# A two-block transformer on one core: where an expert's fetched rows are turned, and where the code behind a branch stands

## The reference, cut to what matters

```python
def moe_swiglu(xn, router, wg, wu, wd):
    t = xn.reshape(B * S, D)                              # 256 x 1024
    top_val, top_idx = lax.top_k((t @ router), TOP_K)      # 2 of 8 experts
    gates = jax.nn.softmax(top_val, axis=-1)
    combine = jnp.sum(jax.nn.one_hot(top_idx, N_EXPERTS) * gates[..., None], axis=1)
    for e in range(N_EXPERTS):                             # 1024 -> 3584 -> 1024
        out = out + combine[:, e:e + 1] * swiglu(t, wg[e], wu[e], wd[e])
    return out

def first_block(x, p, ...):
    for i in range(DEPTH):
        h = h + hybrid_mixer(rmsnorm(h, norm_mix[i]), ...)
        h = h + (swiglu(...) if i % 2 == 0 else moe_swiglu(rmsnorm(h, norm_ffn[i]), ...))
        gate = jax.nn.sigmoid(rmsnorm(h, ple_norm[i]) @ ple_gate[i])
        h = h + gate * (p[i] @ ple_proj[i])
    return rmsnorm(h, final_norm)

def second_block(x, mem, ...):
    for l in range(DEPTH):
        ...                      # block attention, a gated recurrence, memory attention
        x = x + y @ w_out[l]
    return x
```

## Time and profile before

| | |
|---|---|
| median of 3 runs | 1982.92 us (1981.67 to 1983.06) |
| the profiled execution | 1982.62 us |
| its span | 1980.8 us |
| mean granted TensorE clock | 0.993 |
| busy: PE, DVE, ACT | 1923.5, 1518.7, 1229.4 us |

### The profile page before, as it was taken

How to read it: one execution, slowest core, us unless ns; L and a number is a source line. 1 busy time by engine, 2 the same in 40 slices (tenths; PEclk the granted TensorE clock), 3 DMA queues, 4 the chain that set the end, 5 groups by cost and what they waited for, 6 DMA issues and landing times.

```text
span 1980.8 us, 26870 instructions
## 1 busy us (share of the span) xinstructions
PE 1923.5 (97%) x10275; PEld 1632.1 (82%) x10275; DVE 1518.7 (77%) x1478; ACT 1229.4 (62%) x1332; POOL 28.4 (1%) x28
## 2 busy tenths in 40 slices
PE   8999999999899999999999999999998999999999
PEld 7889998887687887878878788787886788887987
DVE  4675555656788888888888888888996865877576
ACT  4554445554677777777777777777776545354442
POOL 0000000000000000000000000000000000000000
PEclk9999999999999999999999999999999999999999
DMA  7717554532799999999999999999995552345321
GB/s 240 255 59 249 188 192 149 164 113 99 280 375 341 391 379 348 381 340 390 379 348 373 361 395 374 359 384 353 396 361 203 170 171 86 128 170 191 128 86 43
DMA packets 246211, 514.63 MB, mean 260 GB/s; under 512 B 12516, under 2 KB 59240, under 8 KB 246120
## 3 DMA queue, kind: packets, MB, share of 16 engines
q1 hardware_dynamic: 242936, 502.77, 70.4%
q0 software_dynamic: 2896, 10.49, 1.3%
q10 hardware_dynamic: 288, 0.11, 0.0%
HBM read 507.56 MB, written 5.77 MB: 259 GB/s over the span
## 4 chain that ended last, share of the span: by engine, by line
PE 81%; DVE 10%; ACT 3%; issue 3%; SPq 2%; DMA 1%; DVEq 0%; ACTq 0%
PE bank L725 25%; PE bank L727 25%; PE bank L726 25%; DVE low L1936 3%; PE bank L1145 1%; DVE low L2533 1%; PE bank L696 1%; PE bank L849 1%; ACT high L1417 1%; SPq L674 1%; SPq L635 1%; DVE at L2738 1%; PE bank L840 1%; ACT high L1620 1%; PE bank L818 1%
## 5 line engine op out<-in xcount | busy, mean ns | idle before, releaser
L2533 DVE TENSOR_TENSOR low<-raw,high 128x2048 fp32r<-128x2048 f32 x336 | 768.4, 2291 | 117.7 <-ACT high L1620 116.8
L1620 ACT ACTIVATE high<-raw 128x2048 fp32r<-128x2048 f32 x336 | 644.7, 1920 | 240.1 <-PE bank L727 238.3
L1936 DVE TENSOR_TENSOR low<-raw,high 128x2048 fp32r<-128x2048 f32 (+1 forms) x138 | 310.5, 2259 | 168.1 <-ACT high L1417 164.4
L1417 ACT ACTIVATE high<-raw 128x2048 fp32r<-128x2048 f32 (+1 forms) x138 | 260.7, 1894 | 167.8 <-PE bank L727 150.3
L725 PE MATMUL bank<-high,xg_hi 128*128 128x512 f32 x896 | 353.7, 395 | 2.7 <-DVE xg_lo L2516 2.3
L727 PE MATMUL bank<-high,xg_lo 128*128 128x512 f32 x896 | 349.5, 390 | 0.0
L726 PE MATMUL bank<-low,xg_hi 128*128 128x512 f32 x896 | 348.9, 389 | 0.0
L725 PE MATMUL bank<-high,xT_hi 128*128 128x512 f32 (+1 forms) x576 | 228.3, 396 | 8.5 <-issue 5.4
L727 PE MATMUL bank<-high,xT_lo 128*128 128x512 f32 (+1 forms) x576 | 222.2, 386 | 0.0
L726 PE MATMUL bank<-low,xT_hi 128*128 128x512 f32 (+1 forms) x576 | 221.8, 385 | 0.0
L725 PE MATMUL bank<-high,hT_hi 128*128 128x512 f32 x536 | 212.7, 397 | 0.0
(11 more groups left out here) (346 smaller groups left out, 2231.5 us busy)
## 6 DMA issues: line engine op xcount, KB each, us to landing
raw<-in_moe_w_gate SPq DMA_DIRECT2D x112, 1024.0 KB, 6.5
raw<-in_moe_w_up SPq DMA_DIRECT2D x112, 1024.0 KB, 6.8
raw<-in_moe_w_down SPq DMA_DIRECT2D x112, 1024.0 KB, 6.6
raw<-in_w_in SPq DMA_DIRECT2D x63, 1024.0 KB, 5.4
raw<-in_w_out SPq DMA_DIRECT2D x20, 1024.0 KB, 5.0
raw<-in_dense_w_gate SPq DMA_DIRECT2D x11, 1024.0 KB, 5.2
raw<-in_dense_w_up SPq DMA_DIRECT2D x11, 1024.0 KB, 5.3
raw<-in_dense_w_down SPq DMA_DIRECT2D x11, 1024.0 KB, 5.0
```

The costliest lines, as they stand in the source:

```text
L1417: act.activation(high[:, slot, 0:k * n], raw[:, raw_slot[piece], 0:k * n], ACT.Copy).then_inc(high_done, 1)
L1620: act.activation(high[:, k % PARTS, :], raw[:, slot, :], ACT.Copy).then_inc(s["high"], 1)
L1936: dve.tensor_tensor(low[:, slot, 0:k * n], src, high[:, slot, 0:k * n].bitcast(F32), ALU.subtract).then_inc(low_done, 1)
L2533: dve.tensor_tensor(low[:, k % PARTS, :], raw[:, at0 + k % slots, :], high[:, k % PARTS, :].bitcast(F32), ALU.subtract).then_inc(s["low"], 1)
```

## The change

The diff has two parts. In the path that fetches rows by DMA, PE turns the next expert's rows one product earlier, between gate 6 and up 6, into banks 1 and 3, which the odd groups' gate and up products use and which are free by then. ACT waits for up 6 (the last reader of the old `xg_hi`) before it writes the new one. Three semaphores of their own replace the shared counters, and an expert has eight turns instead of ten.

```diff
-    return 5 + j if j < GROUPS - 1 else (11 if is_last else 13)
+    return 5 + j if j < GROUPS - 1 or s["by_dma"] else (11 if is_last else 13)
...
-        moe_sems[0].update(turns=10, by_dma=True)
+        rows_turned, rows_high, rows_low = (sem("taken_rows_" + x) for x in ("turned", "high", "low"))
+        moe_sems[0].update(turns=8, by_dma=True)
...
                         if (what, j) == ("gate", 0):
-                            pe.wait_ge(s["tfree"], 1 + half if is_first else s["turns"] * e + 10 - s["turns"] + half)
+                            if is_first or not s["by_dma"]:
+                                pe.wait_ge(s["tfree"], 1 + half if is_first else s["turns"] * e + 10 - s["turns"] + half)
+                            else:
+                                pe.wait_ge(rows_low, 2 * e - 1 + half)
...
                     if j >= 1:
                         turn_hidden(j - 1)
+                    if j == GROUPS - 1 and not is_last and s["by_dma"]:
+                        turn_taken(e + 1)
                     product("up", j)
...
-                    if j == GROUPS - 1 and not is_last:
-                        if s["by_dma"]:
-                            turn_taken(e + 1, s, lambda a: turn_bank(11 + a))
-                        else:
-                            gather(e + 1, s, lambda a: turn_bank(11 + a))
+                    if j == GROUPS - 1 and not is_last and not s["by_dma"]:
+                        gather(e + 1, s, lambda a: turn_bank(11 + a))
...
-            def turn_taken(e, s, bank_for):
+            def turn_taken(e):
...
                 for a in range(2):
-                    b = bank_for(a)
+                    b = bank[1 + 2 * a]
...
-                    last.then_inc(s["tfull"], 1)
+                    last.then_inc(rows_turned, 1)
```

On ACT and DVE `gathered` takes the semaphores and banks as arguments:

```diff
                     if (what, j, half) == ("up", GROUPS - 1, 1) and not is_last:
-                        gathered(s, s["turns"] * e + 10, (7, 6))
+                        if s["by_dma"]:
+                            act.wait_ge(s["used"], first + PER_EXPERT * e + q + 1)
+                            gathered(rows_turned, 2 * e + 1, rows_high, (1, 3))
+                        else:
+                            gathered(s["tfull"], s["turns"] * e + 10, s["thigh"], (7, 6))
...
                     if (what, j, half) == ("up", GROUPS - 1, 1) and not is_last:
-                        gathered(s, 9 * e + 8, (7, 6))
+                        if s["by_dma"]:
+                            gathered(rows_high, 2 * e, rows_low, (1, 3))
+                        else:
+                            gathered(s["thigh"], 9 * e + 8, s["tfree"], (7, 6))
```

```diff
                 with pe.If(over < 1):
                     finish(moe_sems[0])
-                    embedding_in(1)
+                    after_experts()
                 with pe.Else():
...
-                    embedding_in(1)
+                    after_experts()
...
+            def after_experts():
+                embedding_in(1)
+                embedding_out(1)
+                for l in range(LAYERS):
+                    km, vm = ([(name, l, t) for t in range(NT)] for name in ("km", "vm"))
...
                 else:
                     experts()
-                embedding_out(l)
-
-            for l in range(LAYERS):
-                km, vm = ([(name, l, t) for t in range(NT)] for name in ("km", "vm"))
...
                 if l == 0:
+                    embedding_out(0)
```

ACT has the same with `embedding(1)`, `norm_sums("final")` and the loop over the second block's layers. DVE:

```diff
-                counts = (steps, asked, split_no, high_no, mark_no)
+                counts = (steps, asked, split_no, high_no, mark_no, roots)
...
                 with dve.If(over < 1):
                     finish(moe_sems[0])
-                    embedding_in(1)
+                    after_experts()
...
                 if l == 0:
-                    splits(pieces_of["km", l][0])
...
-                attention2(l)
-                hgrn(l)
+                    layer_embedding(0)
+            add_last(LAYERS - 1)
```

More of the change, by code:

```diff
@@ L1705, in all_experts, with embedding @@
                 return over
+            def embedding(l):
+                embedding_in(0) if l == 0 else embedding_in(1, False)
+                splits(pieces_of["pp", l][0])
+                if l == 1:
+                    mem_sums()
+                for j in range(2):
+                    if (l, j) == (0, 1):
+                        norm_high(("mix", 1), (0, 1))
+                    splits(pieces_of["pg", l, j][0])
+                    for t in range(NT):
+                        n = (l * 2 + j) * NT + t
+                        if n >= 2:
+                            act.wait_ge(gate_used, n - 1)
+                        take(("gate", l, j, t), gatebuf[:, n % 2, :], func=ACT.Sigmoid)
+                        if (l, j, t) == (0, 1, 0):
+                            half_squares(("mix", 1), 0)
+                    if j == 0:
+                        splits(pieces_of["pg", l, j][1])
+                    if (l, j) == (0, 1):
+                        sqrt_ahead()
+                        half_squares(("mix", 1), 1)
+                        serve_rstd()
+                        norm_high(("mix", 1), (2, 3))
+                        splits(pieces_of["pg", l, j][1])
+                    if (l, j) == (1, 0):
+                        mem_high(0)
@@ L1800, in _ @@
                         sqrt_ahead()
-                        embedding_in(1, False)
+                        after_experts()
                 if l == 0:
[L1803 to L1827, removed]
@@ L1828, in _ @@
-            norm_sums("final")
-            for l in range(LAYERS):
-                if l == 0:
-                    splits(pieces_of["km", l][0])
[L1832 to L1864, removed]
-                act.activation(flat(qT, 0, 4), a2[:, :], ACT.Silu).then_inc(gates_in, 1)
-                splits(pieces_of["z", l, 0][0])
-                def z_take(i):
-                    for t in range(NT):
-                        n = (l * 3 + i) * NT + t
-                        if n >= 2:
-                            act.wait_ge(z_used, n - 1)
-                        take(("z", l, Z_ORDER[i], t), zbuf[:, n % 2, :], func=ACT.Silu)
-                z_take(0)
-                splits(pieces_of["z", l, 0][1])
-                splits(pieces_of["z", l, 2][0])
-                z_take(1)
-                splits(pieces_of["z", l, 2][1])
-                splits(pieces_of["z", l, 1][0])
-                z_take(2)
-                for j in (0, 1, 4, 5):
-                    rows = xT_hi if j < 4 else yT_hi
-                    high_rows_of(("yT2", l, j), [rows[:, (2 * j + k) % KB, :] for k in range(2)])
-                splits(pieces_of["z", l, 1][1])
-                serve_sqrt(8)
-                splits(pieces_of["wo2", l][1])
-                for j in (2, 3):
-                    high_rows_of(("yT2", l, j), [xT_hi[:, 2 * j + k, :] for k in range(2)])
-                if l == 0:
-                    mem_high(1)
-                splits(last_piece["wo2", l] - 1)
@@ L1895, in _ @@
+                    embedding(0)
         @block.gpsimd
@@ L2519, in gathered @@
                             op0=ALU.mult, op1=ALU.subtract)
-                    last.then_inc(s["tfree"], 1)
+                    last.then_inc(low_part, 1)
             def scattered(s, e, x, parts):
@@ L2809, in hgrn, with add_last @@
                     add_acc("wo2", l)
-                    return
+            def add_last(l):
                 for n in range(4):
```

239 lines of the change are left out of this document (155 added, 84 removed).

## The result

The changed kernel takes 1962.92 us (median of 4 runs, 1960.34 to 1964.04), against 1982.99 us (4 runs, 1981.67 to 1984.22) for the kernel before on the same chip: a ratio of 0.9897, with a 95% interval of 0.988 to 0.9914. The profiled execution has a span of 1961.8 us.

The account below looks back on a forecast made before the run. PE was taken to bound the kernel, so only its idle and low-clock time could be won: 5.5 (pauses) + 6.4 (clock) + 8.0 (branch) = 19.9 us off 1982.6 gives 1962.7, as a median 1963.0; range 1956.5 to 1971.5.

Parts of the forecast that it names:

- Part one: Change of expert: fetched rows turned ahead of up 6 shorten PE's pause from 2.05 to 1.26 us; 0.79 each, 5.5 in all.
- The rival without a pause: Change of expert: the pause goes altogether because DVE runs further ahead; 28.7 us off, 1954.2; chance 0.08.
- The clock: Behind changes of expert: a pause of 1.26 us should keep PE's clock, removing four half-clock stretches of 1.6 us; 6.4 us.
- The branch: Gate product behind the experts: moving the jump to the program's end removes PE's idle times and low clock; 8.0 us.
- the rival by which the idle times aren't the jump's: Behind the branch: idle times come from code fetched in order and stay; 11.9 us off, 1971.0; chance 0.10.
- The end: End of the program: the moved jump costs nothing, its 6.2 us branch instruction ending at 1979.7 with 1.1 us to spare.
- the one named: Program's end: the jump shows, PE done at 1983.1 instead of 1980.8; 2.3 us more, 1965.3, up to 1969; chance 0.12.
- The slower rival: Loop over the experts on PE: its branch back misses its target, six passes at 8.0 us; 28 slower, 2011; chance 0.03.

Follow-up runs that it names:

- e7: Changed kernel with DVE making the low hidden columns ahead of `xg_lo`, and the fetched rows' second bank one piece later on DVE and ACT; 1952.98 us.
- e3: Kernel before, jump kept, with the branch's second arm on PE, ACT and DVE cut to what the first does (no second expert pass); 1974.22 us.
- e2: Kernel before with only the branch part of the change: code behind the experts in both arms, fetched rows turned as before; 1973.22 us.
- e6: Changed kernel with two extra, unread DVE multiplications in front of the low part of the hidden columns at each change of expert; 1979.87 us.
- e1: Kernel before with only the fetched rows' part of the change (turned ahead of up 6), the branch left as it was; 1969.78 us.
- e4: Kernel before with the branch's second arm cut to what the first does on PE only; ACT and DVE still jump far; 1977.44 us.

## Why the prediction was right

The forecast was 1963.0 us; the measured median is 1962.92. Its reasons held, with one step wrong. That the two numbers meet to 0.1 us is luck: the forecast for the profiled execution was 1962.7, and it took 1963.61; the changed kernel's own runs lie 4 us apart; and the wrong step and a piece that has nothing to do with the change nearly cancel.

*Part one.* The forecast saving of 0.79 us per change is 121.1 - 120.39 = 0.7 in the profile. Its reading of what comes next, `hT_lo` as the last of four DVE jobs without a gap, is what the waits and DVE's timeline show. Start to start, the pause is 1355.14 - 1353.58 - 0.23 = 1.33 us, forecast as 1.26. Down 6 starts 1355.14 - 1347.90 = 7.24 us behind up 6, forecast as 7.35. What is missing of the saving is in the first matmuls behind the pause (0.48 and 0.50 us long where 0.39 is usual). 7 x 0.7 = 4.9 stands for 5.5. With the clock's 6.4 that is 11.3, and the experts took 11.0 less. The rival without a pause failed here by DVE's order of work alone, as e7 shows.

*The clock.* "One of 1.26 should keep it": it did, in 28 changes of 28, and four falls at 1.6 us are the 6.4 forecast. The reasoning was sound for the profiled execution. But the number of falls of the same pause was 4, 4, 6 and 6 in four profiles, so the gain differs from run to run. This fits the spread of the kernel before, 1979.2 to 1987.3 us over its 40 runs here, against 1960.3 to 1964.5 for the changed kernel's eight. The 36 of those runs that were made beside the experiments have their mean granted clock on record: it is 0.993 or 0.994 in the eleven under 1981.5 us, and 0.989 to 0.991 in the ten above 1985. How many falls each had is known only for the profiled executions.

*The branch.* Forecast 8.0, measured 8.18. DVE's cover holds, by 1.56 us; the working gave 13.9 - 12.2 = 1.7. e3 shows the jump's distance as the cause; the rival by which the idle times aren't the jump's falls with it. Two readings on the way were wrong. The 3.23 us were held against the Trainium skill's sentence on straight code, and e3 shows them to be the jump's. And the two idle times by "issue" behind the branch are not PE's only ones: there is a third of 1.59 us, 10.4 us into the span, in code that isn't changed; it is 1.77 us in the changed kernel. It weakens the argument against that rival, but not the result of e3.

*The end: the step that failed.* "So it costs nothing, with 1.1 us to spare." It costs 1.3 us, though not in the way of the rival. The branch instruction was short, 3.74 us rather than 6.21, and was over before the last matmul began, at 1953.1 + 3.74 = 1956.8. What I didn't ask is what else the fetch would meet: at the old place it met weight loads, at the new one the last output transfers, which then land 1.1 us later. Of the chain to the end only the landing was left, and I had taken it as fixed. This was not foreseen as a rival either: the one named lets PE itself end late.

*What made up for it:* the span before the experts was 1.05 us shorter, which is no part of the change and differs between executions of the same code. Without both, the profiled execution would be 0.3 us lower: in sum -20.3 + 1.3 = -19.0, where the forecast had -19.9.

*The slower rival:* the loop's branch back took 0.21 us in the median before and after, and at most 0.27 in any of the six passes. Nothing speaks for this rival.

## What to carry to other kernels

A wait removed in front of an engine brings only the distance to the next one in the same producer's order; so write that order out and put first what the bound engine reads first (e7 won 9.9 us more in this way with no work removed). A jump over a long arm cost 2.0 to 6.2 us on each engine here and was cheapest where the engine had nothing left to do, but its fetch is traffic too, and at the end of a kernel the output's landing pays for it. A pause of PE can cost time by the clock as well as by its length: the clock gave back 6.4 us here and the shorter pauses 4.9, so a pause that the clock still falls behind is worth more than it shows.

## What the runs showed of the hardware that I had not expected

- The same jump, with a target more than twice as far, took 6.2 us in the middle of the weight loads (6.21 and 6.24) and 3.5 to 3.8 at the end (3.74 in the changed kernel, 3.82 in e2, 3.53 in e6). The DMA engines were full at the first place, as the DMA view of the kernel before from 1500 to 1512 shows, and mostly idle at the second. That this is the reason is argued, not shown: no run put the jump at a quiet place with the short distance.

```profile
q1 hardware_dynamic: 2265, 4.51, 102.1%
q8 instruction: 2, 0.03, 1.1%
```

- A fetch of 0.03 MB beside output DMAs made these take 3.1 instead of 2.0 us (3.0 in e2). Which resource the two share stays open. The trickle of 14 to 27 GB/s at the end is about a sixteenth of the some 380 that the same view shows while a whole piece of output moves, and a core has 16 DMA engines; so an estimate is that one of them finishes its part of the output late. No view here shows which engine carried the instructions.
- Behind a long jump PE idles twice: 2.2 us at once and 2.5 to 3.2 us three or four matmuls later (2.18 and 2.52 in e1). With a short jump (e3) both are gone.
- With pauses of 1.8 to 2.4 us the clock fell behind some and not behind others of the same length, in the same execution; with pauses of 1.3 us and less it never did. Which of the seven changes had a fall differs: the first four in the kernel before, the first six in e4, all but the fifth in e3 and e6, the first three and the last in e2. What decides it is not shown.
